# Expert matrices loaded as one contiguous 8 KB run per partition, with the contraction order permuted to match

## What is computed

```
    def one_block(args):
        tok_b, gate_b, e = args
        xb = xpad[tok_b]
        hb = jax.nn.silu(xb @ w_gate[e]) * (xb @ w_up[e])
        return (hb @ w_down[e]) * gate_b[:, None]
...
    shared = (jax.nn.silu(hf @ ws_gate) * (hf @ ws_up)) @ ws_down
    x = x + g2[:, None, :] * (routed + shared).reshape(B, L, D)
```

## Time and profile before

| | |
|---|---|
| Three executions | 3219.52, 3226.58 (median), 3230.39 us |
| Profiled execution, first to last instruction (span) | 3224.1 us |
| Share of the span in which PE / DVE / POOL / ACT are busy | 83% / 55% / 36% / 33% |
| Bytes moved by DMA | 518.50 MB, mean 161 GB/s |
| Expert part, from PE's first gate_up matmul to its last gather's transposes | 1216.6 to 3095.2 us of the span |

### The profile page before, as it was taken

How to read it: one execution, slowest core, us unless ns; L and a number is a source line. 1 busy time by engine, 2 the same in 40 slices (tenths; PEclk the granted TensorE clock), 3 DMA queues, 4 the chain that set the end, 5 groups by cost and what they waited for, 6 DMA issues and landing times.

```text
span 3224.1 us, 56738 instructions
## 1 busy us (share of the span) xinstructions
PE 2685.4 (83%) x11753; PEld 2015.7 (63%) x11754; DVE 1778.0 (55%) x3601; ACT 1058.2 (33%) x2213; POOL 1147.3 (36%) x1173
## 2 busy tenths in 40 slices
PE   6897787778777839999999998989999999999940
PEld 1174564555565517877777777777777777777730
DVE  1034785785677754355554466565645544445558
ACT  1022212112111213244443355454534443344411
POOL 0025525644753342323233322223332232232337
PEclk9998898898887769999999999999999999999975
DMA  7751001001000306567776688888887677667665
GB/s 267 294 228 43 30 33 53 20 33 59 7 33 33 121 16 191 116 193 226 220 214 181 187 253 245 230 254 241 252 225 217 194 211 207 182 177 195 174 177 203
DMA packets 255795, 518.50 MB, mean 161 GB/s; under 512 B 18222, under 2 KB 154375, under 8 KB 255588
## 3 DMA queue, kind: packets, MB, share of 16 engines
q1 hardware_dynamic: 199108, 327.34, 29.4%
q0 software_dynamic: 56624, 190.48, 24.7%
HBM read 386.48 MB, written 131.99 MB: 161 GB/s over the span
## 4 chain that ended last, share of the span: by engine, by line
PE 53%; POOL 15%; DMA 12%; issue 10%; DVE 5%; ACT 3%; ACTq 1%; DVEq 1%; POOLq 1%; SPq 0%
PE zb L1465 22%; PE mx L1465 11%; PE zb L1299 7%; POOL b_av L501 7%; DMA b_xg<-hf_d,b_gidx 5%; PE tp L1478 4%; POOL list_d L511 4%; DMA acc_d<-b_ob,b_sidx 3%; PE mx L1321 3%; PE zb L1263 2%; DMA b_big<-in_w_ada 2%; PE zb L1414 1%; ACT b_wh L794 1%; DVE b_wl L1168 1%; POOL b_pa L484 1%
## 5 line engine op out<-in xcount | busy, mean ns | idle before, releaser
L595 POOL DMA_INDIRECT acc_d<-b_ob,b_sidx x180 | 310.8, 1727 | 1067.2 <-DVE b_ob L1193 556.4
L1465 PE MATMUL zb<-b_wh,b_xh 128*128 x1448 | 589.7, 407 | 53.3 <-issue 33.8
L1465 PE MATMUL zb<-b_wh,b_xl 128*128 x1448 | 572.8, 396 | 0.0
L1465 PE MATMUL zb<-b_wl,b_xh 128*128 x1448 | 572.2, 395 | 0.0
L1168 DVE TENSOR_TENSOR b_wl<-b_win,b_wh (+1 forms) x780 | 481.3, 687 | 132.1 <-ACT b_wh L794 131.8
L794 ACT CAST b_wh<-b_win (+1 forms) x780 | 419.8, 621 | 147.0 <-issue 113.3
L1299 PE MATMUL zb<-b_hT,b_win 128*128 128x256 f32 x1536 | 364.9, 402 | 95.6 <-ACT b_sgt L671 94.6
L1299 PEld LDWEIGHTS zb<-b_hT,b_win 128*128 128x128 f32 x1536 | 310.7, 204 | 149.0 <-ACT b_sgt L671 97.4
L903 DVE SCALAR_TENSOR_TENSOR b_y<-b_a_buf,b_wdw,b_y 128x256 f32<-128x256 f32 x960 | 380.7, 481 | 0.0
L1465 PEld LDWEIGHTS zb<-b_wh,b_xh 128*128 128x128 f32 x1448 | 273.5, 189 | 131.3 <-issue 72.6
L1145 DVE SCALAR_TENSOR_TENSOR b_hh<-b_sgx,b_lt,zb 128x256 f32<-128x256 f32 x181 | 86.9, 480 | 477.7 <-ACT b_sgx L779 476.5
(11 more groups left out here) (242 smaller groups left out, 3211.8 us busy)
## 6 DMA issues: line engine op xcount, KB each, us to landing
b_win<-in_w_gate SPq DMA_DIRECT2D x64, 1024.0 KB, 6.3
b_win<-in_w_up SPq DMA_DIRECT2D x64, 1024.0 KB, 12.4
b_win<-in_w_down SPq DMA_DIRECT2D x64, 1024.0 KB, 14.5
b_big<-in_w_ada SPq DMA_DIRECT2D x12, 2048.0 KB, 9.0
acc_d<-b_x1b SPq DMA_DIRECT2D x1, 9216.0 KB, 35.0
b_xin<-in_x_prompt SPq DMA_DIRECT2D x16, 512.0 KB, 3.2
b_big<-in_w_ada_final SPq DMA_DIRECT2D x4, 2048.0 KB, 8.1
b_xres<-in_x_prompt SPq DMA_DIRECT2D x16, 512.0 KB
```

The costliest lines, as they stand in the source:

```text
L595: G.indirect_dma_start(acc_d, bass.IndirectOffsetOnAxis(ap=sidx[1 - j][:, 0:1], axis=0), ob[1 - j][:], None, compute_op=ALU.add).then_inc( ...
L1465: last = M.matmul(o, lhs, rhs, start=(first and n == 0), stop=(final and n == len(terms) - 1))
```

## The change

The three loads of `load_w` give partition p eight neighbouring rows of gate and of up (two of down) where they gave it every 128th row. In DRAM these rows are one run of 8 KB, and the staging area now keeps them as one run too: `stage_w` has, for each half, a part for gate, one for up and one for down, 2048 floats each. Before, gate and up came in rows of 1 KB that were laid beside each other, and down in rows of 4 KB.

A unit of 512 columns is therefore read from two places of the staging area, 256 columns of gate and 256 of up, by the new functions `staged` and `split_w`; `wh` and `wl` keep their layout. Since slice k of a matrix now holds the rows k, k + 8, k + 16 and so on, the transposes of `gx` take every 8th column of `xg`, and those of `ht` every 2nd column of `hh`.

```diff
+    stage_w = win[:].rearrange("p k n -> p (k n)").rearrange("p (s t x) -> p s t x", s=2, t=3)
+    def staged(set_, u):
+        if u < UG:
+            return stage_w[:, ds(set_, 1), 0:2, u * DE:(u + 1) * DE]
+        return stage_w[:, ds(set_, 1), 2:3, (u - UG) * 512:(u - UG + 1) * 512]
+    def split_w(t, set_, u):
+        v = t[:, ds(set_ * UW + u, 1), :]
+        return v.rearrange("p s (g n) -> p s g n", g=2 if u < UG else 1)
...
-            sp.dma_start(stage_gu[:, set_, 0:UG, 0, :], gate.rearrange("(k p) n -> p k n", p=P)).then_inc(S["w_landed"], 16)
-            sp.dma_start(stage_gu[:, set_, 0:UG, 1, :], up.rearrange("(k p) n -> p k n", p=P)).then_inc(S["w_landed"], 16)
-            sp.dma_start(stage_d[:, set_].rearrange("p (k n) -> p k n", k=KE), down.rearrange("(k p) n -> p k n", p=P)).then_inc(S["w_landed"], 16)
+            for part, w in enumerate((gate, up, down)):
+                sp.dma_start(stage_w[:, set_, part, :], w.rearrange("(p k) n -> p (k n)", p=P)).then_inc(S["w_landed"], 16)
...
-                A.copy(wh[:, ds(sn * UW + u, 1), :], stage[:, ds(sn * UW + u, 1), :]).then_inc(S["w_hi"], 1)
+                A.copy(split_w(wh, sn, u), staged(sn, u)).then_inc(S["w_hi"], 1)
...
-                V.tensor_tensor(wl[:, at, :], stage[:, at, :], wh[:, at, :].bitcast(F32), ALU.subtract).then_inc(S["w_lo"], 1)
+                V.tensor_tensor(split_w(wl, sn, u), staged(sn, u), split_w(wh, sn, u).bitcast(F32), ALU.subtract).then_inc(S["w_lo"], 1)
...
-                    last = M.transpose(tp[h][:, kk * P:(kk + 1) * P], xg[j][:, k * P:(k + 1) * P], ident[:])
+                    last = M.transpose(tp[h][:, kk * P:(kk + 1) * P], xg[j][:].rearrange("t (p k) -> t p k", k=KD)[:, :, k], ident[:])
...
-                last = M.transpose(ly[:, k * P:(k + 1) * P], hh[:, k * P:(k + 1) * P], ident[:])
+                last = M.transpose(ly[:, k * P:(k + 1) * P], hh[:].rearrange("t (p k) -> t p k", k=KE)[:, :, k], ident[:])
```

More of the change, by code:

```diff
@@ L139, in program @@
     win = sb("win", [P, KD, DIN])
-    stage = win[:].rearrange("p k n -> p (k n)").rearrange("p (u n) -> p u n", n=512)
+    stage_w = win[:].rearrange("p k n -> p (k n)").rearrange("p (s t x) -> p s t x", s=2, t=3)
[6 more added lines that the diff above has]
+        return v.rearrange("p s (g n) -> p s g n", g=2 if u < UG else 1)
     names = """const_in c_in small_in win_in wout_in state_in bc_in zero_st init_st edge_st xres_in x1_st h2_st smod_in
@@ L276, in _ @@
         shared = [a["ws_gate"][0], a["ws_up"][0], a["ws_down"][0]]
-        stage_gu = stage.rearrange("p (s u) (g n) -> p s u g n", s=2, g=2)
-        stage_d = stage.rearrange("p (s u) n -> p s (u n)", s=2)[:, :, UG * 512:]
         def load_w(set_, gate, up, down):
-            sp.dma_start(stage_gu[:, set_, 0:UG, 0, :], gate.rearrange("(k p) n -> p k n", p=P)).then_inc(S["w_landed"], 16)
-            sp.dma_start(stage_gu[:, set_, 0:UG, 1, :], up.rearrange("(k p) n -> p k n", p=P)).then_inc(S["w_landed"], 16)
-            sp.dma_start(stage_d[:, set_].rearrange("p (k n) -> p k n", k=KE), down.rearrange("(k p) n -> p k n", p=P)).then_inc(S["w_landed"], 16)
+            for part, w in enumerate((gate, up, down)):
+                sp.dma_start(stage_w[:, set_, part, :], w.rearrange("(p k) n -> p (k n)", p=P)).then_inc(S["w_landed"], 16)
         def expert(e):
@@ L1166, in rest_w @@
                     rounded.wait(S["w_hi"])
-                at = ds(sn * UW + u, 1)
-                V.tensor_tensor(wl[:, at, :], stage[:, at, :], wh[:, at, :].bitcast(F32), ALU.subtract).then_inc(S["w_lo"], 1)
+                V.tensor_tensor(split_w(wl, sn, u), staged(sn, u), split_w(wh, sn, u).bitcast(F32), ALU.subtract).then_inc(S["w_lo"], 1)
         front_stored(dve)
```

## The result

The changed kernel takes **3351.89 us** (median; 3350.27 to 3369.35) where the kernel before takes 3225.13: a ratio of **1.0409, 95% interval 1.0382 to 1.0435**. It is slower by some 127 us. The forecast said 3338, with a range of 3225 to 3400, so the number holds. The reasons don't: the largest term of the sum, +157 us for the transposes, measures 0 to 7 us, and what replaces it is what the forecast had as rival B, at nearly three times its price (127 us where 3270 us meant some 45).

A forecast was written before the change was run, and what follows sets the result against it. PE was taken to bound the expert part, busy 1766 of 1879 us. The sum was 3224.1 + 157 (transposes) - 36 (stalls) - 10 (weights) = 3335 us of span, so 3338 as median, with a range of 3225 to 3400.

The forecast's parts named there:

- rival B: PE reads at full speed, but one-for-one queue alternation makes gathers later: 3270 us, 3215 to 3320 around it; chance 0.16.
- Transposes of every 8th column, +157 us: `xg` transposes, 8 a block: 218 ns per weight load instead of 109, 0.87 us a block over 180 blocks; ends 0 to 171.
- the absolute figure: DVE's 1.78 ns per float at a step of 64 floats, times 128: 228 ns for a PE weight load.
- The rule named beside it: SBUF's 16-byte lines need two hits for full speed: a 32-byte step pays, an 8-byte step doesn't; the sum stays.
- `ht`, nothing: Two transposes a block of every 2nd column, 8-byte step: taken as no cost, upper bound 39 us; loads stay at 141 ns.
- Rounding, nothing: Rounding and its rest, reading two runs of 256 floats: no cost, instructions staying at 621 and 687 ns.
- Weights, -10 us: Weight loads in 8 KB packets get 0.8 us shorter, giving back part of ACT's 33.7 us of waits; ends 0 and -34.
- Gathers 1.4 us later: Gathers queued behind a scatter-add, beside 8 KB weight packets passing one for one: 1.4 us later, between 0 and 3.2.
- the stated end of 3.2: Upper end, in us, of how much later a gather could land beside 8 KB packets.
- Stalls, -36 us: PE's stall at late gathers shrinks by 0.8 us in 45 blocks, since PE asks 2.2 us later; ends +45 and -60.
- The slower clock: PE's granted clock, named behind some of the 178 us of stalls in the expert part; no term of its own.
- some 115 ns apart: Transposes starting under this spacing decide for PE reading every 8th float at full speed, queues sharing by bytes: 3193 us, chance 0.14.

## Why the number held and the reasons didn't

- **Transposes of every 8th column, +157 us: the step that failed.** The prediction priced PE by DVE's reductions, near "the absolute figure, since a wait for memory should go by time and not by an engine's clock", and held that "no matmul hides them". The run with the transposes alone puts the cost at 0 to 7 us. What failed is the step from how long a load lasts to how far apart loads start. The load did grow, by about 50 ns, but loads overlap, as the prediction's own rows had it (142 ns long, 109 ns apart). The Trainium skill, "TensorE: Matmul & The Clock Gate", section "Back-to-back issue gap", says that in a stream of pairs of weight load and matmul the spacing of the matmuls is set by both, pipelined; the runs agree in that transposes with loads of 193 to 209 ns start 111 to 119 ns apart. That DVE pays for a step was not shown either: its two reductions differ in their results too, 128 values against 16, and no run parts the two.
- **The rule named beside it.** The Trainium skill, "Advanced Engine Details and Errata", section "Memory Cachelines", has lines of 16 bytes and wants two hits in each, so a step of 32 bytes would pay and one of 8 bytes would not. For PE's weight loads here both steps make the load longer, and the one of 8 bytes more (209 against 193 to 196 ns); neither is paid in full.
- **`ht`, nothing: right in time**, though its weight loads show 199 ns and not the 141 that was to show it.
- **Rounding, nothing: right**, at 621 and 687 ns.
- **Weights, -10 us: right in size, not shown in its path.** Packets take 312 ns (322 forecast), down lands after 12.8 us (under 14 forecast), and ACT's waits are shorter by 33.7 - 23.0 = 10.7 us. But later blocks of PE shorten such waits too. With early gathers the loads alone gain some 10 us while ACT's waits for weights stay (36.8 us in the kernel before, 39.1 with 8 KB loads), so ACT's waits aren't where it comes from.
- **Gathers 1.4 us later: right in mechanism, too small.** The example shows 14.0 - 11.7 = 2.3 us, the longest gather 12.3 - 9.6 = 2.7, inside the stated end of 3.2. The prediction had reckoned that much of a load would have passed before the scatter-add's first packet.
- **Stalls, -36 us: wrong in sign**, because PE's longer blocks, which were to absorb the later gathers, never came, and the gathers came later than reckoned. The waits grew by 62.8 + 24.6 - 17.2 = 70.2 us.
- **The slower clock: missing from the sum.** 56.6 us of busy time, nearly half the loss. The prediction read "the slower clock behind some" of the stalls in the trace and gave it no price for longer ones. How much of the 127 us the clock takes by itself wasn't tried in a run of its own; the split is read from the busy time.

Rival B named the mechanism ("the one-for-one alternation makes gathers later"), at 3270 us with 3320 as its upper end. It missed the clock. That the sum ended 14 us from the measured time is luck: a term of +157 us that doesn't exist stood in for waits of +70 us and a slower clock of +57 us, which the sum had at -36 and at nothing. The price that decided for the transposes, "some 115 ns apart", was read rightly: they start 111 ns apart, and the sign then did hang on the gathers.

## What to carry to other kernels

Where two DMA queues alternate packet by packet, as here, the packet size of the bulk queue acts as a priority: larger packets made the bulk shorter and the small, urgent transfer later. Before paying for that with smaller packets, look at when the urgent transfer is issued: here it stood one turn behind a scatter-add in program order, and moving the scatter-add one turn later made the larger packets a small gain. And price an operand's access pattern by the distance between starts in the same engine's trace, not by the duration of one instruction or by another engine.

## What the runs showed of the hardware

- PE's weight load of 128 x 128 floats lasts 141 ns with neighbouring columns, 209 ns at a step of 2 or 4 floats and 193 to 196 ns at 8 to 32; the transposes start 109, 119 and 113 ns apart.
- Queues alternate one for one also where the packets are 8 KB and 4 KB (87 and 84 in 3.5 us), so that the larger ones get two thirds of the bytes.
- After a wait of 2.5 us, eight transposes and 1.9 us of idle time, 12 matmuls took 5.46 us in place of 2.79, at a granted clock of 0.50. In the kernel before, the late gather of the earlier trace rows cost a wait of 0.2 us and 1.0 us of idle time, and the clock stayed at 1.00.
